# MLP up products of a four-layer transformer kernel: block products of two by two with seven products in place of eight

## The reference

```
def squared_relu_mlp(h, w_up, w_down):
    return jnp.square(jax.nn.relu(h @ w_up)) @ w_down
...
x = x + squared_relu_mlp(rms_norm(x, mlp_norm[layer]), w_up[layer], w_down[layer])
```

## Time and profile before

| | us |
|---|---|
| median of 3 runs | 2100.04 |
| lowest, highest | 2094.2, 2104.07 |
| span of the profiled execution | 2099.7 |

### The profile page before, as it was taken

One profiled execution on the slowest core, in us unless ns is written; L12 is line 12 of the kernel. 1 busy time (PEld: TensorE's weight loads), 2 busy tenths in 40 slices (PEclk: granted clock), 3 DMA queues, 4 the chain that ended last, 5 costly groups with the idle time before them and its releaser, 6 DMA issues.

```text
span 2099.7 us, 28844 instructions
## 1 busy us (share of the span) xinstructions
PE 2076.6 (99%) x11148; PEld 1645.5 (78%) x11148; DVE 947.6 (45%) x1431; ACT 933.3 (44%) x1477; POOL 759.2 (36%) x316
## 2 busy tenths in 40 slices
PE   8999999999999999999999999999999999999999
PEld 5777788888888886668888888778788887877887
DVE  7875552112137256765211212667733354773331
ACT  7642453323236326774322324556742344765231
POOL 3332144444444630003444444344034443402443
PEclk9999999999999999999999999999999999999999
DMA  4442133333332431002333333232022333201232
GB/s 155 134 123 70 45 104 99 92 101 91 94 99 88 146 96 31 2 14 92 100 91 101 91 101 101 74 97 81 12 81 90 91 93 94 85 22 61 91 100 81
DMA packets 62710, 178.96 MB, mean 85 GB/s; under 512 B 17776, under 2 KB 18160, under 8 KB 62592
## 3 DMA queue, kind: packets, MB, share of 16 engines
q1 hardware_dynamic: 47600, 168.04, 26.3%
q10 hardware_dynamic: 14992, 9.22, 1.6%
HBM read 171.97 MB, written 3.70 MB: 84 GB/s over the span
## 4 chain that ended last, share of the span: by engine, by line
issue 48%; PE 34%; POOL 16%; ACT 1%; POOLq 0%; DMA 0%; SPq 0%; DVE 0%
POOL w_lo L2709 16%; PE banks L760 9%; PE banks L762 9%; PE banks L761 9%; PE banks L1282 1%; PE banks L1295 1%; PE banks L1267 1%; PE banks L811 1%; PE banks L1273 1%; PE banks L1239 0%; DMA x<-in_x 0%; PE banks L1330 0%; POOLq L2715 0%; POOLq L2717 0%; PE banks L1331 0%
## 5 line engine op out<-in xcount | busy, mean ns | idle before, releaser
L2709 POOL TENSOR_TENSOR w_lo<-raw,w_hi 128x1024 fp32r<-128x1024 f32 (+1 forms) x312 | 759.0, 2434 | 1322.8 <-ACT w_hi L1415 1322.7
L760 PE MATMUL banks<-h_lo,w_hi 128*128 128x512 f32 (+1 forms) x1408 | 567.0, 403 | 9.3 <-POOL w_lo L2709 9.3
L762 PE MATMUL banks<-h_hi,w_hi 128*128 128x512 f32 (+1 forms) x1408 | 554.7, 394 | 0.0
L761 PE MATMUL banks<-h_hi,w_lo 128*128 128x512 f32 (+1 forms) x1408 | 551.5, 392 | 0.0
L1415 ACT ACTIVATE w_hi<-raw 128x1024 fp32r<-128x1024 f32 (+1 forms) x312 | 327.9, 1051 | 489.4 <-PE banks L762 456.5
L760 PEld LDWEIGHTS banks<-h_lo,w_hi 128*128 128x128 f32 (+1 forms) x1408 | 264.4, 188 | 73.8 <-POOL w_lo L2709 8.7
L761 PEld LDWEIGHTS banks<-h_hi,w_lo 128*128 128x128 f32 (+1 forms) x1408 | 264.5, 188 | 62.2 <-issue 4.8
L762 PEld LDWEIGHTS banks<-h_hi,w_hi 128*128 128x128 f32 (+1 forms) x1408 | 264.3, 188 | 60.7 <-issue 0.7
L760 PE MATMUL banks<-a_lo,w_hi 128*128 128x512 f32 x768 | 304.5, 397 | 0.0
L762 PE MATMUL banks<-a_hi,w_hi 128*128 128x512 f32 x768 | 301.6, 393 | 0.0
L761 PE MATMUL banks<-a_hi,w_lo 128*128 128x512 f32 x768 | 299.8, 390 | 0.0
(11 more groups left out here) (365 smaller groups left out, 2466.5 us busy)
## 6 DMA issues: line engine op xcount, KB each, us to landing
raw<-in_weights SPq DMA_DIRECT2D x311, 512.0 KB, 3.6
x<-in_x SPq DMA_DIRECT2D x4, 512.0 KB, 6.2
AT<-row_dram ACTq DMA_DIRECT2D x4, 512.0 KB, 7.6
out<-x SPq DMA_DIRECT2D x8, 256.0 KB, 2.6
eg<-row_dram ACTq DMA_DIRECT2D x8, 128.0 KB, 3.3
phase<-in_phase ACTq DMA_DIRECT2D x1, 706.0 KB, 4.9
phase<-in_phase ACTq DMA_DIRECT2D x1, 704.0 KB, 4.2
ld_dram<-Ld ACTq DMA_DIRECT2D x1, 512.0 KB, 5.4
```

The costliest lines, as they stand in the source:

```text
L760: mm(out, w_hi, x_lo, start=first, stop=False)
L761: mm(out, w_lo, x_hi, start=False, stop=False)
L762: return mm(out, w_hi, x_hi, start=False, stop=last)
L2709: return nc.gpsimd.tensor_tensor(c.w_lo[:, slot, 0:n], c.raw[:, slot, 0:n], c.w_hi[:, slot, 0:n].bitcast(F32), ALU.subtract)
```

## The change

An up product is cut in blocks of two by two: a pair of output tiles (two times 128 rows), a pair of input tiles, and the tokens in two halves of 256. The eight block products of such a cell become seven, each between sums of weight tiles and sums of inputs, and the outputs are sums of the seven (Winograd's form). Two stream blocks hold a pair of output tiles (`g`), each with two cells' weights. Three of the seven weight operands, and with them `raw_s`, `w_hi_s`, `w_lo_s`, are new:

- VectorE makes four sums of 256 columns from each up block (`weight_sums`). For a quarter's first three blocks this is done in the stage before, for the others between the steps of `mlp`.
- ScalarE converts `raw_s` (768 columns) ahead of `raw`, after waiting for the sums; GpSimd makes `w_lo_s` ahead of `w_lo`.
- TensorE runs 42 matmuls of 256 columns per block (`seven`), two products in a bank, four banks for a pair of output tiles and the other four for the next.
- ScalarE copies product p1 out of PSUM (`first`); VectorE makes seven adds of 256 columns, then `rectified` in place, in SBUF, for both tiles. ScalarE's squares and roundings of pair g-1 stand behind the weights of pair g.
- Ahead of the first quarter the inputs' sums (`input_sums`) and their low parts (`pair_lo`, `sums_lo`) are made per pair of tiles, in place of `h_hi` and `h_lo`. On ScalarE `pair_hi` rounds the two tiles' three used halves, `sums_hi` the four sums (1024 columns in one operation).
- The loops of SP and GpSimd over the stream are written out.

```
+W_S1, W_11, W_12, W_22, W_S2, W_S3, W_S4 = range(7)
+X_11, X_21, X_22, X_T1, X_T2, X_T3, X_T4 = range(7)
+SEVEN = [("p1", W_11, X_11), ("p2", W_12, X_21), ("p6", W_S2, X_T2), ("p3", W_S4, X_22), ("p7", W_S3, X_T3),
+         ("p5", W_S1, X_T1), ("p4", W_22, X_T4)]
+SUM_BLOCK = 2 * P
...
+        splits(*[(part, 2 * layer + 1, i) for i in range(PAIRS) for part in ("hx", "ht")])
         for q in range(FF_PARTS):
-            each("up", layer, q, n=KT)
+            for g in range(PAIRS):
+                block[("up", layer, q, g)] = (at_block(2), 0)
+                for n, (name, _, _) in enumerate(SEVEN):
+                    b = 4 * (g % 2) + n // 2
+                    if n % 2 == 0:
+                        beside[("up", layer, q, g, b)] = uses[b]
+                    take(("up", layer, q, g, name), b, n % 2 == 1)
...
+    def seven(layer, q, g, half, first):
+
+        b = block[("up", layer, q, g)][0] + half
+        pe.wait_ge(c.w_lo_ready, b + 1)
+        for n, (name, w, x) in enumerate(SEVEN):
+            key = ("up", layer, q, g, name)
+            bnk, hi, lo, at = bank[key][0], *weight_block(w)
+            if half == 0 and n % 2 == 0:
+                pe.wait_ge(c.bank_read[bnk], beside[("up", layer, q, g, bnk)])
+            out = c.psum[bnk][:, n % 2 * HALF:n % 2 * HALF + HALF]
+            for k in range(2):
+                i, cols = 2 * half + k, slice(at + k * P, at + k * P + P)
+                if first:
+                    pe.wait_ge(c.split_lo, split[("ht" if x >= X_T1 else "hx", 2 * layer + 1, i)] + 1)
+                w_hi, w_lo, x_hi, x_lo = hi[:, b % RING, cols], lo[:, b % RING, cols], c.hs_hi[:, i, x, :], c.hs_lo[:, i, x, :]
+                mm(out, w_hi, x_lo, start=half == k == n % 2 == 0, stop=False, skip_group_check=True)
+                mm(out, w_lo, x_hi, start=False, stop=False, skip_group_check=True)
+                ins = mm(out, w_hi, x_hi, start=False, stop=half == k == 1, skip_group_check=True)
+            if n == len(SEVEN) - 1:
+                ins.then_inc(c.block_used, 1)
+            elif half and n % 2:
+                ins.then_inc(c.bank_filled[bnk], 1)
+
     def mlp(layer):
         n = 2 * layer + 1
         for q in range(FF_PARTS):
-            for m in range(KT):
-                gemm(("up", layer, q, m), h_hi, h_lo, needs=parted("h", n) if q == m == 0 else None)
-                if q == m == 0:
+            for g in range(PAIRS):
+                seven(layer, q, g, 0, q == g == 0)
+                if q == g == 0:
                     norm_sum(n)
+                seven(layer, q, g, 1, q == g == 0)
...
+            if b in sums:
+                act.wait_ge(c.weight_sums, sums.index(b) + 1)
+                f(c.w_hi_s[:, b % RING, :], c.raw_s[:, b % RING, :], ACT.Copy)
             f(c.w_hi[:, b % RING, 0:n], c.raw[:, b % RING, 0:n], ACT.Copy).then_inc(c.w_hi_ready, 1)
...
+            for m in (2 * g, 2 * g + 1):
+                key = ("a", layer, q, m)
+                act.wait_ge(c.relu_ready, (layer * FF_PARTS + q) * KT + m + 1)
+                act.wait_ge(c.split_lo, split[key] - 2)
+                step(f(c.stage[:, split[key] % 3, :], c.relu[:, m % 2, :], ACT.Square))
+                hi(key, c.a_hi[:, m, :])
+
...
-            for m in range(KT):
-                up, key, i = ("up", layer, q, m), ("a", layer, q, m), (layer * FF_PARTS + q) * KT + m
-                passed(*up)
-                read(up)
-                act.wait_ge(c.split_lo, split[key] - 2)
-                step(f(c.stage[:, split[key] % 3, :], c.relu[:, i % 2, :], ACT.Square))
-                hi(key, c.a_hi[:, m, :])
+            for g in range(PAIRS):
+                key = ("up", layer, q, g, "p1")
+                weights(block[key[:4]][0] + 2)
+                if g:
+                    squared(q, g - 1)
+                weights(block[key[:4]][0] + 3)
+                f(c.first[:, g % 2, :], filled((*key[:4], "p2"))[:, 0:HALF], ACT.Copy).then_inc(release(key), 1)
+            squared(q, PAIRS - 1)
             if q < FF_PARTS - 1:
...
+    def weight_sums(b):
+
+
+        slot = b % RING
+        part = [c.raw[:, slot, n * SUM_BLOCK:(n + 1) * SUM_BLOCK] for n in range(4)]
+        part += [c.raw_s[:, slot, n * SUM_BLOCK:(n + 1) * SUM_BLOCK] for n in range(3)]
+        dve.wait_ge(c.raw_loaded[slot], 16 * (b // RING + 1))
+        tt_op(part[W_S3], part[W_11], part[W_S1], ALU.subtract)
+        s1 = marked(tt_op(part[W_S1], part[W_S1], part[W_22], ALU.add))
+        yield
+        after(s1)
+        s2 = marked(tt_op(part[W_S2], part[W_S1], part[W_11], ALU.subtract))
+        yield
+        after(s2)
+        tt_op(part[W_S4], part[W_12], part[W_S2], ALU.subtract).then_inc(c.weight_sums, 1)
+        yield
...
+    def input_sums(n, i):
+
+        g1, g2 = [norm_gain(c, pa, n, 2 * i + s) for s in range(2)]
+        x1, x2, t = c.x[:, 2 * i, :], c.x[:, 2 * i + 1, :], c.t_sum
+        x_final(dve, c, bank, n, 2 * i)
+        x_final(dve, c, bank, n, 2 * i + 1)
+        if n == 3 or i:
+            dve.wait_ge(c.split_lo, split[("ht", n, i - 1)] + 1 if i else split[("ht", 1, PAIRS - 1)] + 1)
+        v.tensor_scalar(c.part[:, 0, :], x1[:, 0:HALF], g1, None, ALU.mult)
+        gained = marked(v.tensor_scalar(c.part[:, 1, :], x1[:, HALF:T], g1, None, ALU.mult))
+        after(gained)
+        t1 = marked(tt_op(t[:, 0, :], c.part[:, 1, :], c.part[:, 0, :], ALU.subtract))
+        stt(t[:, 2, :], x2[:, HALF:T], g2, c.part[:, 1, :], ALU.mult, ALU.subtract)
+        after(t1)
+        t2 = marked(stt(t[:, 1, :], x2[:, HALF:T], g2, t[:, 0, :], ALU.mult, ALU.subtract))
+        after(t2)
+        stt(t[:, 3, :], x2[:, 0:HALF], g2, t[:, 1, :], ALU.mult, ALU.subtract).then_inc(c.t_ready, 1)
...
+        for m in range(KT):
+            add_to_x((*key, m), m)
+            if m:
+                norm_add(n, m)
+            if m % 2:
+                input_sums(n, m // 2)
+            if m % 2 == 0 and m:
+                pair_lo(n, m // 2 - 1)
+                sums_lo(n, m // 2 - 1)
+            b = block[(*key, m)][1] + RING
+            if b >= first and (m == KT - 1 or block[(*key, m + 1)][1] + RING > b):
+                all_sums(b)
+        norm_add(n, KT)
+        pair_lo(n, PAIRS - 1)
+        sums_lo(n, PAIRS - 1)
...
+        def rectified(m):
+            y = c.relu[:, m % 2, :]
+            stt(y, y, 0.0, r, ALU.max, ALU.mult).then_inc(c.relu_ready, 1)
...
+            for g in range(PAIRS):
+                first = block[("up", layer, q, g)][0]
+                end = block[("up", layer, q, PAIRS - 1)][0] + 2
+                ahead = [weight_sums(b) if b < end else iter(()) for b in (first + RING, first + RING + 1)]
+                key = {name: ("up", layer, q, g, name) for name, _, _ in SEVEN}
+                y1, y2, p1 = c.relu[:, 0, :], c.relu[:, 1, :], c.first[:, g % 2, :]
+
+                def out(name, with_name):
+                    n = [name for name, _, _ in SEVEN].index(name)
+                    return filled(key[with_name])[:, n % 2 * HALF:n % 2 * HALF + HALF]
+
+                if g:
+                    low(q, 2 * g - 2)
+                next(ahead[0], None)
+                if g:
+                    low(q, 2 * g - 1)
+                next(ahead[0], None)
+                next(ahead[0], None)
+                read(key["p1"])
+                tt_op(y1[:, 0:HALF], out("p2", "p2"), p1, ALU.add).then_inc(release(key["p2"]), 1)
+                tt_op(c.part[:, 0, :], out("p6", "p3"), p1, ALU.add).then_inc(release(key["p6"]), 1)
+                read(key["p6"])
+                tt_op(c.part[:, 1, :], out("p7", "p5"), c.part[:, 0, :], ALU.add).then_inc(release(key["p7"]), 1)
+                u4 = marked(tt_op(c.part[:, 2, :], out("p5", "p5"), c.part[:, 0, :], ALU.add))
+                read(key["p7"])
+                tt_op(y2[:, HALF:T], out("p5", "p5"), c.part[:, 1, :], ALU.add).then_inc(release(key["p5"]), 1)
+                after(u4)
+                tt_op(y1[:, HALF:T], out("p3", "p3"), c.part[:, 2, :], ALU.add).then_inc(release(key["p3"]), 1)
+                next(ahead[1], None)
+                read(key["p3"])
+                rectified(0)
+                dve.wait_ge(c.block_used, first + 2)
+                tt_op(y2[:, 0:HALF], c.psum[bank[key["p4"]][0]][:, 0:HALF], c.part[:, 1, :], ALU.add).then_inc(release(key["p4"]), 1)
+                next(ahead[1], None)
+                read(key["p4"])
+                rectified(1)
+                next(ahead[1], None)
+            low(q, KT - 2)
+            low(q, KT - 1)
...
+                    b = block[("down", layer, q, m)][1] + RING
+                    if b in sums:
+                        all_sums(b)
...
-            with sp.Fori(1, n_blocks // RING) as turn:
-                for slot in range(RING):
-                    sp.wait_ge(c.w_lo_ready, (turn - 1) * RING + slot + 1)
-                    sp.dma_start(c.raw[:, slot, :], in_weights[turn * RING + slot]).then_inc(c.raw_loaded[slot], 16)
```

(38 more changed lines are left out.)

96 lines of the change are left out of this document (71 added, 25 removed).

## The result

The changed kernel takes **2258.52 us** (median of 4 runs, 2258.2 to 2260.21), the kernel before beside it on the same chip 2099.92. The ratio is **1.0756, 95% interval 1.0738 to 1.0774**: 158.6 us slower. The forecast was 2262, in the range 2184 to 2335; forecast and sign held. The span of the profiled execution is 2258.3 us, against 2099.7 before: the same 158.6 us.

What follows compares the result with a forecast made beforehand. The prediction took TensorE's matmul columns to bound the old kernel, and serial preparation on VectorE, ScalarE and GpSimd the new one. 2099.7 + 133 (eight quarters) + 30 (layer starts) = 2263, called 2262 us, range 2184 to 2335.

Steps and rivals of the forecast that it cites:

- The bound: Up blocks: TensorE's matmul columns bound the old kernel, 5.49 us a block, about 2.0 us free in the weight split.
- The products: Up products on TensorE: 2688 matmuls of 256 columns at 124 ns, 333 us from 351.4, 5.21 us a block.
- The durations: Operations in up blocks: w_hi_s 0.81 us, w_lo_s 1.96, VectorE's sums and PSUM adds 0.42 each.
- The meetings: VectorE operations with two SBUF inputs take turns with GpSimd on the shared port: 12.7 us per pair of blocks.
- The series: Up blocks: VectorE, ScalarE, GpSimd work serially, 18.3 us per pair from 10.98; up quarter 58.2 us, +14.3.
- TensorE idle before blocks 3 to 7: Expected sign in up quarters of about 58 us: TensorE waits before each of these blocks.
- seam: From an up quarter to the down quarter: last a_lo 7.1 us after the products, 2.3 us late.
- The layer starts: Start of both MLPs: VectorE's added work, 45 us in all, stalls TensorE; +30 us for both, bounds 10 and 45.
- The sum: Whole kernel: 2099.7 + 133 for eight quarters + 30 for layer starts = 2263, called 2262 us; chance 0.63.
- Rival 1: Up quarters: serial steps overlap, a pair costs the shared port's 12.7 us; total 2184 us, chance 0.17.
- Rival 2: Up blocks: TensorE's idle pauses drop the clock to 1.2 GHz; 2322 us, or 2380 and more; chance 0.12.
- Rival 3: Up blocks: lead and overlap hide all preparation if below 10.4 us a pair; 2090 us, chance 0.08.

Runs made afterwards that it cites:

- the run without sums: Changed kernel with VectorE's weight sums left out behind each layer's first three blocks, ScalarE not waiting for them (wrong result): 2106.2 us, ratio 1.0039.
- long memsets: Changed kernel with three chained memsets, about as long, in place of each GpSimd subtraction in up blocks (low parts zero): 2154.9 us, ratio 1.0257.
- the best order: Changed kernel, whole computation reordered: w_hi waits for one sum, w_hi_s and w_lo_s later, second block's sums early, a_lo late, ScalarE's tiles before weights: 2167.1 us, ratio 1.0305.
- fewer input operations: Changed kernel with six VectorE input operations per pair of tiles at layer starts replaced by two writing scaled tiles (wrong result): 2244.8 us, ratio 1.07.
- the first block's sums first: Changed kernel with the weight sums of each pair's first block made ahead of the a_lo subtractions: 2194.3 us, ratio 1.0459.
- the added products: Changed kernel with twelve extra 256-column products ahead of the weight wait, from each up quarter's fourth block on: 2261.8 us, ratio 1.0761.
- memsets: Changed kernel with GpSimd's two subtractions per up block replaced by single memsets of the same columns (low parts zero): one run, 2137.8 us.
- long memsets with the first order: Changed kernel with three chained memsets per GpSimd up-block subtraction (low parts zero) and second block's sums made before VectorE's first product read: 2093.2 us, ratio 0.9976.

## Why the prediction was right

- **The bound.** It read that eight blocks of 5.49 us leave the other engines 2 us each, and that TensorE's saving needs a block every 5.2. Confirmed by the run without sums: with 1.7 us of VectorE's work gone, the blocks come at 4.9 to 5.0 us.
- **The products.** Taken at 124 ns, measured mostly 113 to 120 ns inside a block (544.24 to 544.36 with w_hi_s, 547.31 to 547.42 with w_hi), nearer to the lower end that the 64-column row gave. The sign "120 to 127 ns apart" was missed; in the changed kernel the miss costs nothing, since the products are hidden, as the step said.
- **The durations.** w_lo_s 1.96, measured 1.89; w_hi_s 0.81, 0.84; sums 0.42, 0.41 to 0.43 where nothing holds them; additions 0.42, 0.41 to 0.43.
- **The meetings.** Operations with two SBUF inputs take turns with GpSimd, those with a bank do not: the first sum 410 to 2668 ns, the addition 423 to 427. The long memsets show that these meetings, and not GpSimd's length, make the 105 us.
- **The series.** Blocks 3 to 7 were to start at 17.7, 26.3, 34.7, 44.6 and 53.0; measured 17.3, 25.6, 33.7, 43.1 and 51.3, in every quarter behind a layer's first alike (the last quarter of layer 1 ends 1.5 us later, by its slow last block). The four late intervals came out at 8.3, 8.1, 9.4 and 8.2, for 8.6, 8.4, 9.9 and 8.4. The sign "TensorE idle before blocks 3 to 7" held for 4 to 7 alone: the early waiting lies before blocks 1 and 2 (starts at 5.8 and 12.3), and block 3 follows without a stop. Quarter +12.4 for +14.3, seam +2.4 for +2.3: eight quarters 118 for 133, 15 us too much. GpSimd is busy 33.6 us of an up quarter, for about 35. The wait of the seam is seen: TensorE waits for an a_lo 15 times, 13.0 us in all.
- **The layer starts** came to 37 for 30, inside the bounds of 10 and 45, and in part for another reason than the volume given. The predicted stop of some 15 us in the first block of layer 0 came as 20.8 us ahead of it. VectorE is busy for 17.4 of these (columns as in the earlier trace rows), held time included, so its work is most of the stop. The rest is waiting, as these rows of VectorE at its end show, and one of ScalarE:

```profile
296.67:317.43 20.76, 0.40 (x2) 0.03 (x1) 17.37 (x23) 7.46 (x13) 8.83 (x4) 0.58 0.15 50
...
311.18 1.28 DVE L2173 TENSOR_TENSOR norm<-norm,sq 128x512 f32<-128x512 f32 x1 [2.47 <-ACT sq L1571]
312.38 3.22 DVE L2249 SCALAR_TENSOR_TENSOR hs_lo<-x,params,hs_hi 128x256 fp32r<-128x256 f32 x2
315.52 1.21 DVE L2255 TENSOR_TENSOR hs_lo<-t_sum,hs_hi 128x1024 fp32r<-128x1024 f32 x1
316.66 0.68 DVE L2194 TENSOR_TENSOR x<-x,banks 128x512 f32<-128x512 f32 x1
...
308.22 0.84 ACT L1496 ACTIVATE w_hi_s<-raw_s 128x768 fp32r<-128x768 f32 x1 [8.94 <-DVE raw_s L2219]
```

  The first up product needs a bank that the addition of the last x tile reads (316.66). That addition stands on VectorE behind the low parts of the pair before, these behind a norm addition that waits 2.47 us for a square, and the square stands on ScalarE behind w_hi_s, which waits 8.94 us for VectorE's own sums. Two engines wait for each other in turn. Swapping ScalarE's order gives 6 to 7 us, fewer input operations as much; the two were not run together, and the rest of the 37 us was not taken apart.
- **The sum** was right to 4 us in part by luck, because the errors cancel: -15 in the quarters, +7 at the starts, +3 ahead of the first MLP that are not the change's. Each term by itself was near, 133 for 118 and 30 for 37.
- **Rival 1, the port alone,** 2184: refuted for this order, but it is where order leads; the best order ran at 2167. It is below 2184 because an up and a down quarter are together 4 us over those before, where the rival had 6.7. The series on top of the port, with 6 us of the layer starts, cost 95 us.
- **Rival 2, the clock:** its condition came true and its price did not. TensorE's timeline around one pause:

```profile
547.65 0.28 PE L903 MATMUL banks<-hs_hi,w_hi 128*128 128x256 f32 x1
551.11 0.39 PE L901 MATMUL banks<-hs_lo,w_hi 128*128 128x256 f32 x1 [3.19 <-POOL w_lo L2951]
...
551.57 0.28 PE L901 MATMUL banks<-hs_lo,w_hi 128*128 128x256 f32 x1
551.69 0.28 PE L902 MATMUL banks<-hs_hi,w_lo 128*128 128x256 f32 x1
...
552.79 0.41 PE L901 MATMUL banks<-hs_lo,w_hi_s 128*128 128x256 f32 x1
553.00 0.41 PE L902 MATMUL banks<-hs_hi,w_lo_s 128*128 128x256 f32 x1
```

  After 3.46 us without a start the products first run 0.12 us apart, then 0.21, the pace of 1.2 GHz. In layer 1 twice as much time is at the low clock (0.88 against 0.94 in the windows above) and the quarter is as long. The Trainium skill (TensorE: Matmul & The Clock Gate, "HAM oscillation — how this bites in real kernels") says that idle gaps throttle the clock and that this costs. The first half is seen here. The second is not in the blocks that a wait follows, since the next block's weights set its start, and it is in the last block of the last quarter, with 1.5 us. The rival's own argument against it was right: the slow products use up idle time. Before blocks 4 to 7 of this quarter TensorE is idle for 3.2, 1.5, 4.2 and 1.5 us, not 3.2 to 4.7 before each.
- **Rival 3, faster:** the condition (preparation below 10.4 us a pair) holds only with the sums gone or with port and order both free, and even then the time was 2106 and 2093, not clearly below the kernel before: the layer starts take back what the quarters give.

## What to carry to other kernels

Trading matmul columns for elementwise work pays only if that work finds a place in the other engines' order and in the port that VectorE and GpSimd share: sums of 1.7 us a block cost 18 to 19 us for each up quarter of eight blocks, with the down quarter behind it and its share of the layer starts. Price each added operation by what waits behind it, followed once through all engines' programs, and count VectorE's operations with two SBUF inputs together with GpSimd's subtractions as one resource; GpSimd's memsets did not belong to it here. An order can be worth more than the columns saved (95 us here, where the saved columns gave 4 to 5 us a quarter at best), and a fallen clock beside a wait is first to be read as a symptom; ask whether a wait follows the slow stretch, for without one it does cost.

## What the runs showed of the hardware that was not expected

- The 256-column stream is not of one pace: in the block before the pause above, products with w_hi_s stood 0.120 us apart (544.24 to 546.28, 17 steps), those with w_hi 0.114 (546.40 to 547.65, 11 steps), and whole quarters without stops took 39.0 or 39.9 us. Why, stays open.
- The granted clock fell in windows where it had not before, also outside the MLP. The pause of the earlier trace rows grew from 2.47 to 3.49 us between starts, and the same window now reads 0.87 in place of 1.00:

```profile
119.15 0.40 PE L812 MATMUL banks<-h_hi,w_hi 128*128 128x512 f32 x1
122.64 1.19 PE L861 MATMUL banks<-sq,phase 128*128 128x512 f32 x1 [3.09 <-ACT sq L1535]
...
115.00:125.00 10.00, 6.91 (x24) 4.64 (x23) 9.42 (x22) 8.53 (x11) 0.96 (x1) 0.87 0.00 0
```

  The change does not touch this stretch, and the variants of the changed kernel, which have the same program there, differ too. The idle time of this pause was 1.77 us with the long memsets, 2.09 with the first block's sums first, 3.09 above and 3.25 with the added products. The clock of the window stayed 1.00 with 1.77 and in the kernel before with 2.08, and read 0.86 with 2.09. From this `sq,phase` group to the next it is 3.70 us where the window reads 1.00 and 5.2 and 5.3 in the changed kernel and with the first block's sums first (6.4 with the added products): a fall costs 1.5 us here. Why the pause has another length in another execution stays open.
- Products of 512 columns in the MLPs of the last two layers stand 233 ns apart in the kernel before and the changed one, and 229 in the profile with fewer input operations, at a granted clock of 1.00 in the changed kernel and this one. With it the part of the span behind the second MLP is 755 us where it was 761, and in three other profiles (memsets, long memsets with the first order, added products) 754. Why, stays open.
